# Token and channel sums on VectorE, with one sum over the partitions left on TensorE, in a hybrid mLSTM and convolution layer

## The reference

```python
# mLSTM, per head (4 heads, DK = 256, DV = 512); q, k, v, gates from the input projection
s   = einsum('bthk,bshk->btsh', q, k) * w_intra          # masked, weighted scores
num = einsum('btsh,bshv->bthv', s, v) + w_inter * einsum('bhvk,bthk->bthv', C, q)
den = jnp.sum(s, axis=2) + w_inter * einsum('bhk,bthk->bth', n, q)
h   = num / jnp.maximum(jnp.abs(den), jnp.exp(-m_t))
n_new = dec * n + einsum('bsh,bshk->bhk', wk, k)         # the normaliser
# convolution branch
c = depthwise_conv(u) + b_dw
mu = mean(c, axis=-1); xc = c - mu                       # layernorm over 1024 channels
c = silu(xc * rsqrt(mean(xc * xc, axis=-1) + EPS) * g + b)
```

## Time and profile before

| what | us |
|---|---|
| median of 3 runs | 1310.61 (1309.87 to 1311.29) |
| profiled execution, its own time | 1310.51 |
| its span | 1308.7 |
| TensorE busy | 1255.0 (96%) |
| VectorE busy | 721.6 (55%) |
| ScalarE busy | 507.5 (39%) |
| TensorE's granted clock, mean | 0.982 of full |

### The profile page before, as it was taken

How to read it: one execution, slowest core, us unless ns; L and a number is a source line. 1 busy time by engine, 2 the same in 40 slices (tenths; PEclk the granted TensorE clock), 3 DMA queues, 4 the chain that set the end, 5 groups by cost and what they waited for, 6 DMA issues and landing times.

```text
span 1308.7 us, 23730 instructions
## 1 busy us (share of the span) xinstructions
PE 1255.0 (96%) x9099; PEld 1175.6 (90%) x9099; DVE 721.6 (55%) x970; ACT 507.5 (39%) x750; POOL 74.6 (6%) x135
## 2 busy tenths in 40 slices
PE   6999899999999999999999999997799999999994
PEld 6999877888797888879999999997799999999993
DVE  4252588978878888884455443337443212444324
ACT  5333343353354334334554222235554223554211
POOL 3011201100100110110000000000000000000002
PEclk8999899999999999999999999998899999999997
DMA  6235716514441651531222222430232222222211
GB/s 191 81 110 167 108 33 221 191 49 151 174 166 42 218 189 42 186 136 65 81 97 81 97 80 80 149 99 32 80 96 97 81 95 81 81 96 82 95 48 68
DMA packets 39761, 141.17 MB, mean 108 GB/s; under 512 B 5012, under 2 KB 5524, under 8 KB 39592
## 3 DMA queue, kind: packets, MB, share of 16 engines
q1 hardware_dynamic: 27848, 99.37, 23.8%
q0 software_dynamic: 11872, 41.23, 9.5%
HBM read 118.31 MB, written 22.26 MB: 107 GB/s over the span
## 4 chain that ended last, share of the span: by engine, by line
PE 89%; DVE 4%; ACT 3%; DMA 2%; issue 1%; POOLq 0%; POOL 0%; ACTq 0%; DVEq 0%; SPq 0%
PE product L1311 83%; PE side L1311 6%; DMA wraw<-in_wstream 2%; DVE y L1225 0%; ACT whi L511 0%; DVE sqs L1250 0%; DVE yc L1241 0%; DVE hr L1130 0%; DVE y L1239 0%; DVE crg L1107 0%; DVE wlo L846 0%; DMA x<-in_xT 0%; DVE alo L1235 0%; ACT L674 0%; ACT L524 0%
## 5 line engine op out<-in xcount | busy, mean ns | idle before, releaser
L846 DVE TENSOR_TENSOR wlo<-wraw,whi 128x1024 fp32r<-128x1024 f32 x176 | 215.4, 1224 | 239.8 <-ACT whi L511 234.8
L1311 PE MATMUL product<-ahi,whi 128*128 128x256 f32 x1520 | 320.6, 293 | 18.6 <-DVE fr L1269 7.6
L1311 PE MATMUL product<-ahi,wlo 128*128 128x256 f32 x1520 | 316.8, 290 | 0.0
L1311 PE MATMUL product<-alo,whi 128*128 128x256 f32 x1520 | 315.1, 289 | 0.0
L511 ACT ACTIVATE whi<-wraw 128x1024 fp32r<-128x1024 f32 x176 | 184.5, 1052 | 237.7 <-PE product L1311 177.5
L1311 PEld LDWEIGHTS product<-ahi,whi 128*128 128x128 f32 x1520 | 246.2, 191 | 25.7 <-issue 25.0
L1311 PEld LDWEIGHTS product<-alo,whi 128*128 128x128 f32 x1520 | 245.7, 190 | 0.0
L1311 PEld LDWEIGHTS product<-ahi,wlo 128*128 128x128 f32 x1520 | 245.1, 190 | 0.0
L997 DVE SCALAR_TENSOR_TENSOR accp<-u,wdw,accp 128x512 f32<-128x512 f32 x240 | 163.0, 744 | 0.3
L1311 PE MATMUL product<-hidhi,wlo 128*128 128x256 f32 (+1 forms) x512 | 106.0, 288 | 0.0
L1311 PE MATMUL product<-hidlo,whi 128*128 128x256 f32 (+1 forms) x512 | 105.9, 288 | 0.0
(11 more groups left out here) (260 smaller groups left out, 1660.0 us busy)
## 6 DMA issues: line engine op xcount, KB each, us to landing
wraw<-in_wstream SPq DMA_DIRECT2D x176, 512.0 KB, 3.3
crg<-in_c_in POOLq DMA_DIRECT2D x32, 512.0 KB, 5.8
out_c_s<-crg POOLq DMA_DIRECT2D x32, 512.0 KB, 2.9
hb<-head_rows POOLq DMA_DIRECT2D x4, 580.0 KB, 5.5
x<-in_xT SPq DMA_DIRECT2D x4, 544.0 KB, 5.6
sgm<-in_xT SPq DMA_DIRECT2D x1, 2176.0 KB, 9.0
out_yT<-y SPq DMA_DIRECT2D x8, 272.0 KB, 2.1
out_c_p<-cst POOLq DMA_DIRECT2D x4, 512.0 KB, 7.8
```

What stands on the lines that cost most here:

```text
L846: V.tensor_tensor(wlo[:, k % RING, :, :], wraw[:, k % 2, :, :], whi[:, k % RING, :, :].bitcast(f32), ALU.subtract).then_inc(lo_done, 1)
L1311: return pe.matmul(out, lhsT, rhs, start=start, stop=stop, skip_group_check=check)
```

## The change

In each head VectorE adds the three later pieces of `pt` to one tile, `sqacc`, and TensorE sums 128 columns of `pt` and 384 of `sqacc` in place of four pieces. VectorE reduces `kw` over its four token tiles into `hr[:, 1]`, and TensorE sums its two halves with one matmul each. Behind the heads VectorE adds the eight convolution tiles into `mu`, and TensorE sums that once. In the gate loop ScalarE's square moves ahead of the sigmoid, and TensorE's sum of the squares moves behind the first product of the next eight.

```diff
@@ scalar, the gate loop
                     j = 4 * i + k
+                    act.wait_ge(xc_ready, j + 1)
+                    squares(j + KT, tile(u, j), k % 2)
                     act.wait_ge(chunk_done, 4 * i + (C_GATE + k + 1))
                     act.activation(tile(sgm, j), slot(k % 2), ACT.Sigmoid, bias=c("b_gm", j)).then_inc(drained[k % 2], 1)
-                    act.wait_ge(xc_ready, j + 1)
-                    squares(j + KT, tile(u, j), k % 2)
@@ vector, in a head behind the second sampled products
+                    if s_ == 3:
+                        dve.wait_ge(pt_ready, 5 * h + 5)
+                        w = mark(V.tensor_tensor(sqacc[:, P:SEQ], pt[:, P:SEQ], pt[:, PT_AT[1]:PT_AT[2]], ALU.add))
+                        dve.wait_ge(dve_step, w)
+                        w = mark(V.tensor_tensor(sqacc[:, 2 * P:SEQ], sqacc[:, 2 * P:SEQ], pt[:, PT_AT[2]:PT_AT[3]], ALU.add))
+                        dve.wait_ge(dve_step, w)
+                        V.tensor_tensor(sqacc[:, 3 * P:SEQ], sqacc[:, 3 * P:SEQ], pt[:, PT_AT[3]:N_PT], ALU.add).then_inc(wsum_ready, 1)
@@ vector, in a head behind the vst subtraction
+                dve.wait_ge(kt_used, ST * h + ST)
+                V.tensor_reduce(hr[:, 1, 0:DK], kw[:, :, :].rearrange("p q k -> p k q"), X, ALU.add).then_inc(ksum_ready, 1)
@@ vector, behind the heads
-            V.memset(sqs[:, :], 0.0).then_inc(conv_ready, 1)
+            n = mark(V.memset(sqs[:, :], 0.0))
+            for j in range(1, KT):
+                first = u[:, 0, 0:TT] if j == 1 else mu[:, :]
+                dve.wait_ge(dve_step, n)
+                ins = V.tensor_tensor(mu[:, :], first, u[:, j, 0:TT], ALU.add)
+                if j < KT - 1:
+                    n = mark(ins)
+                else:
+                    ins.then_inc(conv_ready, 1)
@@ tensor, in a head
                 pe.wait_ge(pt_ready, 5 * h + 5)
-                for q in range(ST):
-                    ins = mm(side[:, 0, P * q:SEQ], ones[:, :], pt[:, PT_AT[q]:PT_AT[q] + SEQ - P * q], q == 0, q == ST - 1)
-                ins.then_inc(den_ready, 1)
+                pe.wait_ge(wsum_ready, h + 1)
+                mm(side[:, 0, 0:P], ones[:, :], pt[:, 0:P], True, True)
+                mm(side[:, 0, P:SEQ], ones[:, :], sqacc[:, P:SEQ], True, True).then_inc(den_ready, 1)
...
                 pe.wait_ge(sden_abs, h + 1)
+                pe.wait_ge(ksum_ready, h + 1)
                 for kk in range(QT):
-                    for q in range(ST):
-                        ins = mm(side[:, 2, P + kk:P + kk + 1], kw[:, q, P * kk:P * (kk + 1)], ones[:, 0:1], q == 0, q == ST - 1)
+                    ins = mm(side[:, 2, P + kk:P + kk + 1], hr[:, 1, P * kk:P * (kk + 1)], ones[:, 0:1], True, True)
@@ tensor, behind the heads
                 if k == 1:
                     pe.wait_ge(conv_ready, 1)
-                    for j in range(KT):
-                        for g in range(2):
-                            ins = mm(piece(side[:, 2:4, :], g), ones[:, :], u[:, j, slice(*PARTS[g])], j == 0, j == KT - 1)
-                    ins.then_inc(mean_ready, 1)
+                    column_sums(mu, 2).then_inc(mean_ready, 1)
             with pe.Fori(1, KT // 4) as i:
                 for k in range(4):
                     alternate(i, k, C_GATE, S_GATE, ahi, alo)
-            pe.wait_ge(sq_added, 2 * KT)
-            column_sums(sqs, 0).then_inc(stat_ready, 1)
-            with pe.Fori(0, KT // 4) as i:
+            for k in range(4):
+                alternate(0, k, C_GATE + KT, S_GATE + KT // 2, ahi, alo)
+                if k == 0:
+                    pe.wait_ge(sq_added, 2 * KT)
+                    column_sums(sqs, 0).then_inc(stat_ready, 1)
+            with pe.Fori(1, KT // 4) as i:
                 for k in range(4):
                     alternate(i, k, C_GATE + KT, S_GATE + KT // 2, ahi, alo)
```

More of the change, by code:

```diff
@@ L92 @@
 PV_TAPS = [(24, 24), (24, 26), (26, 26), (26, 26)]
-DVE_PER_HEAD = 81
+DVE_PER_HEAD = 83
 class Steps:
@@ L294, in hybrid_layer @@
         np_ready, np_used, nn_ready = sem("np_ready"), sem("np_used"), sem("nn_ready")
+        wsum_ready, ksum_ready = sem("wsum_ready"), sem("ksum_ready")
         conv_ready, mean_ready, xc_ready, cn_ready, csg_ready = (sem(n) for n in (
```

## The result

The changed kernel takes 1317.26 us, median of 8 runs (1313.47 to 1319.92), against 1309.13 (1303.29 to 1311.29) for the kernel before in its 8 runs: a ratio of 1.0066, 95% interval 1.0045 to 1.0087. It is slower by 8.6 us, and the forecast of 1311.1 with its range up to 1315.2 missed it. The profiled execution took 1317.13 us (span 1315.4), 6.7 us of span more than before.

The account below looks back on a forecast made before the run. TensorE, nine tenths of the chain that ended last, was taken as the bound. Denominators 0, normaliser -2.6, mean +1.65, clock +2.2 and squares -0.7 gave +0.55 on 1310.5, so 1311.1 us; range for 8 in 10: 1306.5 to 1315.2.

Parts of the forecast that it names:

- Denominators, 0: In each head: TensorE gives up 1.4 us, but chunk 8's low half and a table load take it back; value 0.
- Normaliser, -2.6: Four heads: sums shrink by 1.38 us, 0.72 remains before chunk o2, less 0.07 at o1; 0.65 a head, -2.6 in all.
- the reduction of 992: 1.18, so 1.22: VectorE's normaliser reduction in each head: 1024 elements priced at 1.22 us from a profiled reduction of 992 at 1.18.
- rival A: Normaliser's strided reduction is slow: at 2.36 us chunk o1 waits in each head, -2.6 becomes +1.9, total 1315.6; chance 0.13.
- the edge at which it decides: First state update in each head: its slack before chunk o1 ends when the reduction costs 1.15 us.
- each further us of the reduction would go straight on the path: In each head, at chunk o1: with the reduction at 1.22 us o1 is 0.07 late, and any more delays TensorE directly.
- Mean, +1.65: Behind the heads: the sum ends 4.1 us earlier, but gate chunk 2 waits for square, table load and sigmoid: +1.65.
- Clock behind it +2.2: Behind the heads: after 5.8 us idle before gate chunk 2, TensorE's clock falls and costs 2.2 us.
- squares -0.7: Channel norm's squares, once: the moved sum ends the 2.24 us wait but brings 2.4 idle before the third conv-gate chunk; -0.7.
- half-and-half: Stretch of the squares' sum: 51.5 us, or 53.2 if the clock falls again, weighed equally to give -0.7.
- the forecast without the reduction: The terms behind the heads: mean +1.65, clock +2.2, squares -0.7.
- Rival D: Whole kernel: all work and waits removed from TensorE count, 21.3 us, so 1289.2; chance 0.05.

Follow-up runs that it names:

- e12_short: Kernel before plus, in each head, a reduction of as many elements that reads neighbours, its result unused: 1310.12 us, ratio 1.0021.
- e9_strides: Kernel before plus five reductions of 1024 elements in VectorE's idle time behind the heads, at five strides: 1.16, 1.22, 1.99, 1.88 and 1.97 us each.
- e11_delay: Kernel before plus the strided reduction in each head, its result unused, TensorE's work untouched: 1317.66 us against 1308.09, ratio 1.0079.
- e5_order: e4_late with ScalarE's old order behind the heads, gate sigmoid first and square after it: 1303.13 us against 1310.37, ratio 0.9946.
- e4_late: Changed kernel with the strided reduction moved behind the first two state updates and the low half of chunk 12: 1308.25 us against 1307.89, ratio 1.0005.
- e7_square: Kernel before with ScalarE's order alone changed, the square ahead of the gate sigmoid: 1314.60 us, ratio 1.0033.
- e8_stat: Kernel before with the sum of the squares alone moved behind the first product of the next eight: 1307.97 us against 1308.09, ratio 0.9994.
- e3_adds: Changed kernel with the strided reduction replaced, at the same place, by two adds that read neighbours: 1316.56 us, ratio 1.0063.
- e10_slot: e5_order with ScalarE's first sigmoid of the second gates ahead of the reciprocal root: 1298.97 us against 1308.09, ratio 0.9924.
- e2_norm: Kernel before with the normaliser's part alone, one strided reduction on VectorE and two matmuls: 1314.42 us, ratio 1.0051.

## Why the prediction was wrong, point by point

**Denominators, 0: right.** The adds took 0.55, 0.43 and 0.29 us, 1.27 for 1.35 taken. The wait in front of chunk o0 is the low half of chunk 8, as written, and the table load gives the rest back. What the text didn't count is that such waits may help to bring the clock down; 3 of 16 heads against 0 of 24 hint at it and don't show it.

**Normaliser, -2.6: wrong, and the step that failed is "the reduction of 992: 1.18, so 1.22".** It took 2.05. The price came from rows that read neighbours, and rival A had said so; at twice the price A made it 1315.6, and the edge at which it decides was right in kind: o1 started at 14.6 behind A, 1.1 late. The edge itself lay lower than the 1.15 us written: a reduction of 1.22 made o1 0.3 late in e12_short and not 0.07, so by that run the slack ended near 0.9 us (an estimate). A rule had spoken for A. The Trainium skill, "SBUF — State Buffer", Door 1: The DMA port swizzle, says that accesses that leave a 16-byte line each pay, and that two hits on a line are needed for full speed. e9_strides agrees: two fp32 apart make two hits on a line and took 1.22, four apart make one and paid in full, 1.99, as 16 and 256 apart did. Only the page's own figure, that four fp32 apart are free, isn't borne out. A chance of 0.13 was too little for a mechanism with a rule for it and no row against it.

The other half of the failure is a size: "each further us of the reduction would go straight on the path". It went on the path more than once. The reduction makes o1 late by 1.1, and 0.72 of the normaliser's saving did come back ahead of o2 (2.00 us from the second-last outer product to o2, 2.71 before). Those two alone would be 0.4 a head. The measured 2.4 a head holds a clock that fell in chunk o1, 1.5, in three heads, and readouts that wait for a state's DMA, 0.28 and 0.62, as its load is issued behind an update that is late. These terms together give 6.6 of the 7.3 us of the three heads; the rest isn't assigned. e11_delay shows the late o1 and the fall of the clock without any saving beside them, and 0.18 of such a readout wait in one head.

**Mean, +1.65: right.** Measured +1.35, with the wait of 5.92 in front of chunk 2 of the gates ended by the sigmoid and the table load directly before it. The 0.3 between is one term, the running sum, which repeated each 0.76 us, not 0.83. What the forecast took as a price that had to be paid was a choice: e5_order, with the old order, is by the ratios 7.7 us below e4_late.

**Clock behind it +2.2, squares -0.7: right in sum, by two misses that cancel.** From chunk 2 to the convolution's output the trace has +1.5, the value of both. But the clock behind the 5.92 cost only some 1.3: the seven products from 607.74 to the squares' sum at 651.03 took 43.29 us, against 7 x 5.99 = 41.95 at full clock. The squares' part then cost 0.2 to 0.3 where 0.7 was to be won. So that this stage came out is luck. The clock was at 1.2 GHz for most of 607 to 611, and it fell again behind the wait of 2.40 (granted 0.66 over 661 to 666), the worse half of the half-and-half:

```profile
607.00:611.00 4.00, 3.26 (x16) 3.29 (x17) 1.86 (x2) 1.86 (x3) 0.00 (x0) 0.55 0.08 11
...
661.00:666.00 5.00, 5.00 (x30) 5.00 (x30) 3.99 (x6) 3.39 (x6) 0.00 (x0) 0.66 0.33 105
```

**The whole.** The parts measured one by one give +1.0, +6.7, -5.6, +4.3 and -0.8 us (denominators, normaliser, mean, ScalarE's order, squares' sum), 5.6 in all, and the change 8.6. The difference of 3.0 is within the scatter of so many ratios (some 5 us, taken together). Taking the order away gained 7.7 where adding it alone cost 4.3; that difference of 3.4 is just outside its scatter of 3.3. e7_square and e8_stat together suggest a reason. With the new order the squares' sum needs no wait where it stood (e7_square); moved behind the next product it brings the wait of 2.40 for nothing, and at times a slow clock, 1.7: the clock fell there in the profiled executions of the changed kernel, e3_adds and e8_stat, and not in those of e4_late and e5_order. In the change the move would thus cost 2.4 to 4.1 us more than the 0 it costs by itself. That is read from rows and was not run as a pair. For the profiled stretch the forecast without the reduction still holds, +3.15 against +2.85. Rival D is answered too: e10_slot, which takes away both orders that the change brought in, still gets 9.9 of its 21.3 us, as the denominators give nothing in either order.

## What to carry to other kernels

Before VectorE is given a reduction, look at how far apart it reads: 16 bytes cost 1.7 times as much as neighbours here. Put it where the row behind it has idle time in front, not where an engine's queue leads without a gap to the release of a PSUM slot; the reduction alone cost 10 us at one place, and in the changed kernel moving it down the queue, behind two state updates, gave 8 us back. When an order of two instructions is turned, ask which of them frees a slot: the square needed the mean, the sigmoid didn't, and it held TensorE for 5.9 us. A short wait isn't always free: with one of 0.13 to 1.3 us at a chunk the clock was at half for 3.4 us in 12 of 20 heads. And look whether a loop body that has grown loads its code again at each turn, as in e3_adds: the row of the instruction queues says so.

## What the runs showed of the hardware

A reduction over elements 1, 2, 4, 16 and 256 fp32 apart took 1.16, 1.22, 1.99, 1.88 and 1.97 us: a step between 8 and 16 bytes, and flat behind it. TensorE's clock fell after waits of 0.77, 0.65 and 0.96 us with matmuls and short sums between them; in e2_norm it fell after a single one of 1.22 us, and in e10_slot with none at the chunk that ran slowly. In the heads it gave back full speed after some 3.4 us at 1.2 GHz each time, 1.5 us of time lost in a chunk. Behind the heads the table load of 1.28 at 605.59 was followed by the sigmoid at 606.88; the drain of 1.38 that the Trainium skill, "ScalarE: Activation LUTs", What ACT_TABLE_LOAD costs, adds to a switch isn't there either. The idle time of 3.1 to 3.4 us at each turn of the loop in e3_adds, with the releaser named "issue", went with packets on the instruction queue q14, which no other kernel here has in its loop.
